# Recurrent mixer: where the projection pieces stand among the five levels of a pair's inversion

## The reference

```python
r, k, v, wd, ad = jnp.split(pf, [W, 2 * W, 3 * W, 3 * W + DECAY_LORA], axis=-1)
w = -jax.nn.softplus(-(w0 + jnp.tanh(wd) @ w2)) - 0.5
decay = jnp.exp(-jnp.exp(w))
a = jax.nn.sigmoid(a0 + ad @ a2)
...
def step(state, inp):                      # 512 steps, 16 heads of 64
    sa = jnp.einsum('bhij,bhj->bhi', state, a_t)
    state = state * w_t[:, :, None, :] + sa[..., None] * b_t[:, :, None, :] + v_t[..., None] * k_t[:, :, None, :]
    return state, jnp.einsum('bhij,bhj->bhi', state, r_t)
...
y = ((y - mean) * lax.rsqrt(var + RWKV_GN_EPS)).reshape(B, S, W) * ln_w + ln_b
```

## Time and profile before

| what | us |
|---|---|
| median of 3 runs (3125.1 to 3125.4) | 3125.38 |
| the profiled execution | 3124.12 |
| its span in the profile | 3122.3 |
| TensorE busy in the span | 3085.4 (99%) |
| VectorE busy | 1768.3 (57%) |
| ScalarE busy | 1274.4 (41%) |

### The profile page before, as it was taken

One profiled execution on the slowest core, in us unless ns is written; L12 is line 12 of the kernel. 1 busy time (PEld: TensorE's weight loads), 2 busy tenths in 40 slices (PEclk: granted clock), 3 DMA queues, 4 the chain that ended last, 5 costly groups with the idle time before them and its releaser, 6 DMA issues. The chain is left out here.

```text
span 3122.3 us, 51762 instructions
## 1 busy us (share of the span) xinstructions
PE 3085.4 (99%) x21393; PEld 2539.7 (81%) x21393; DVE 1768.3 (57%) x3073; ACT 1274.4 (41%) x2328; POOL 215.4 (7%) x170
## 2 busy tenths in 40 slices
PE   8999999999999999999999999999999999999999
PEld 6877777777778778788888888888888888888787
DVE  5335565656666754644457776335556656665822
ACT  4124343434434422524346665323344434443521
POOL 0000000001011101000111121110000000000000
PEclk9999999999999999999999999999999999999999
DMA  8433333342232353343331213534223323332452
GB/s 252 126 81 92 91 88 98 100 115 61 67 98 71 108 176 108 112 106 104 107 102 55 61 55 119 162 108 118 88 81 95 95 75 101 95 95 82 161 164 79
DMA packets 494639, 324.25 MB, mean 104 GB/s; under 512 B 27194, under 2 KB 449693, under 8 KB 494406
## 3 DMA queue, kind: packets, MB, share of 16 engines
q1 hardware_dynamic: 494374, 320.94, 35.1%
q10 hardware_dynamic: 32, 0.01, 0.0%
HBM read 276.05 MB, written 44.85 MB: 103 GB/s over the span
## 5 line engine op out<-in xcount | busy, mean ns | idle before, releaser
L550 DVE TENSOR_TENSOR WLT<-AR,WHT 128x1024 fp32r<-128x1024 f32 (+1 forms) x430 | 527.2, 1232 | 655.7 <-ACT WHT L544 654.9
L562 PE MATMUL PS<-XH,WHT 128*128 128x512 f32 (+1 forms) x2224 | 888.3, 399 | 2.7 <-DVE AR L1045 1.4
L564 PE MATMUL PS<-XH,WLT 128*128 128x512 f32 (+1 forms) x2224 | 867.5, 390 | 0.0
L544 ACT ACTIVATE WHT<-AR 128x1024 fp32r<-128x1024 f32 (+1 forms) x430 | 447.5, 1043 | 597.5 <-PE PS L564 464.1
L563 PE MATMUL PS<-XL,WHT 128*128 128x512 f32 (+1 forms) x1712 | 666.9, 390 | 0.0
L562 PEld LDWEIGHTS PS<-XH,WHT 128*128 128x128 f32 (+1 forms) x2224 | 416.3, 187 | 99.1 <-issue 9.3
L564 PEld LDWEIGHTS PS<-XH,WLT 128*128 128x128 f32 (+1 forms) x2224 | 416.0, 187 | 91.0
L563 PE MATMUL PS<-ARR,WHT 128*128 128x512 f32 x1024 | 398.6, 389 | 0.0
L563 PEld LDWEIGHTS PS<-XL,WHT 128*128 128x128 f32 (+1 forms) x1712 | 320.5, 187 | 66.0 <-issue 2.4
L563 PEld LDWEIGHTS PS<-ARR,WHT 128*128 128x128 f32 x1024 | 192.4, 188 | 39.4 <-issue 0.2
L562 PE MATMUL PS<-XL,WHT 128*128 128x512 f32 x512 | 199.7, 390 | 0.4 <-issue 0.4
(11 more groups left out here) (512 smaller groups left out, 5152.6 us busy)
## 6 DMA issues: line engine op xcount, KB each, us to landing
AR<-b_w_in SPq DMA_DIRECT2D x128, 512.0 KB, 4.0
AR<-w_in SPq DMA_DIRECT2D x122, 512.0 KB, 3.9
AR<-a_w_in SPq DMA_DIRECT2D x48, 512.0 KB, 4.6
AR<-w_out SPq DMA_DIRECT2D x32, 512.0 KB, 4.2
AR<-a_w_out SPq DMA_DIRECT2D x32, 512.0 KB, 3.9
AR<-b_w_out SPq DMA_DIRECT2D x32, 512.0 KB, 4.0
proj_scratch<-AR SPq DMA_DIRECT2D x33, 256.0 KB, 2.1
residual_scratch<-RES SPq DMA_DIRECT2D x8, 1024.0 KB, 6.1
```

The source lines that it names most:

```text
L544: self.nc.scalar.activation(self.shaped(self.high, n), self.shaped(self.raw, n), ACT.Copy).then_inc(self.s_high, 1)
L550: self.nc.vector.tensor_tensor(self.shaped(self.low, n), self.shaped(self.raw, n), f32(self.shaped(self.high, n)), ALU.subtract).then_inc( ...
L562: mm(out, wh, xh[k0 + c], start=(start and c == 0), stop=False)
L564: last = mm(out, wl, xh[k0 + c], start=False, stop=(stop and c == nk - 1))
```

## The change

The two pieces of level 2 go to level 3 and the two of level 4 to level 5. Levels 3 and 5 then have four pieces each, levels 2 and 4 none. The pieces keep their order and number. Nothing else is changed; pairs 6 and 7 keep their own lists.

```diff
-            full = {"start": (0, 1, 2, 3), "x2": (4, 5), "x3": (6, 7), "x4": (8, 9), "x5": (10, 11), "solved": (12,), "h": (13,), "s3": (14, 15)}
+            full = {"start": (0, 1, 2, 3), "x3": (4, 5, 6, 7), "x5": (8, 9, 10, 11), "solved": (12,), "h": (13,), "s3": (14, 15)}
             PIECES = [dict(full) for _ in range(NPAIR - 2)]
             PIECES[0].update(start=(), x1=(0, 1, 2, 3))
```

## The result

| | before | after |
|---|---|---|
| median of 4 runs, us | 3125.39 (3125.1 to 3125.51) | 3157.06 (3156.02 to 3158.87) |
| profiled execution | 3124.12 | 3157.46 |
| its span | 3122.3 | 3155.7 |

The change makes the kernel slower: ratio 1.0102, 95% interval 1.0087 to 1.0118, +31.7 us. Forecast were +18.3 us and a range that ended at 3149.5. The sign was right, the size was not.

The account below looks back on a forecast made before the run. TensorE, busy 99% of the span, was taken to bound the kernel. Moved pieces and new waits for ScalarE summed over pairs 0 to 5 to +18.3 us, giving 3143.7 us, with a range of 3135 to 3149.5.

Parts of the forecast that it names:

- What bounds the kernel: TensorE, busy 99% of the span and idle only 2.87 us in pairs 0 to 5.
- the price of a level: Products to sums of a level on TensorE: 1.16 us with no pieces, 4.02 with two, 6.75 with four.
- Level 2: Bare, its second decay waits for ScalarE's `yc`: products to products 4.60 us instead of 6.17 in pairs 1 to 4.
- Level 4's wait: Bare, line 1599 waits for ScalarE's `sga` until 4.49 us after the products, a 2.35 us stall in pairs 2, 4, 5.
- Nothing gives time back later: Level 5 with four pieces costs +2.73 us; what follows moves along unchanged and gives nothing back.
- The sum of the waits: Pairs 0 to 5 together become 18.3 us longer, between +1.86 and +4.03 us per pair.
- rival 5: Longer stalls halve TensorE's clock for four pieces in each pair: +5.5 us per pair, 33 in all, 3177 us; 2%.
- Rivals 1 to 3: Only level 4's wait real, 3136.6 us (8%); only level 2's, 3130.6 (5%); no waits, fewer shape changes, 3123.5 (5%).
- Rival 4: An unseen further wait, or ScalarE and VectorE work bunching in bare levels: 0.5 to 2 us more per pair, 3152; 8%.

Follow-up runs that it names:

- the seven fillers: Changed kernel plus seven unused 128x512 matmuls before line 1599's wait in level 4 of pairs 0 to 5: 3152.23 us, ratio to before 1.0081.
- the mirror: Kernel before with four pieces each in levels 2 and 4, none in levels 3 and 5: 3137.83 us against 3127.11, ratio 1.0033.
- the gate sigmoid later: Changed kernel with ScalarE's early-tile gate sigmoid in level 4 moved behind the sigmoid that line 1599 waits for: 3150.31 us, ratio to before 1.0068.

## Why the prediction was wrong

**What bounds the kernel, and the price of a level: right.** Bare 1.16 to 1.17 us, four pieces 6.75.

**Level 2: right.** 4.60 and 4.61 us in pairs 1 to 4, 5.27 in pair 5, 3.50 in pair 0, each as computed. (The sums of pair 5, 0.9 us late, were not foreseen and cost nothing.) Half of the change alone gave +5.9 against +6.3.

**Level 4's wait: right in place and length.** Line 1599 starts 4.48 to 4.49 us after the products in pairs 2, 4 and 5, 3.97 in 1 and 3 (computed 4.49 and 3.97), 4.56 in pair 0 (4.68). Taking `sga` forward removed it.

**Nothing gives time back later: right.** From the sums of level 5 to the next pair's first product it is 27.7 us in pairs 1, 3 and 4, before and after.

**The sum of the waits, +18.3: right,** shown by pairs 1 and 3 and by the seven fillers (+18.35, where a measure that scatters by half a us makes the last digits luck).

**The step that failed is rival 5, the clock, at 2%:** in the sum the clock's price stood at nothing. That the clock leaves 1.00 was among the prediction's own signs of being wrong, and it is the one that came. It added 13.3 us, in four of six pairs. I dismissed it with one row, that pair 6 keeps its clock with 3.76 us idle in 47. A mean over 47 us and one instance say little about single waits. Pair 6 itself, whose pieces no run touches, has a fall in 8 of the 13 traces. And the trace of before had a counterexample in it: the fall that begins at 1282.95, behind a wait of 1.0 us, and lasts through one of 1.8 us, both no longer than those that I was about to add six times before line 1599. I never looked for it because the clock of 1.00 was read as a mean. The price that I gave it, 5.5 us in each pair, was too high even for a pair that falls: 2.5 to 4.4 us beyond the forecast wait were measured. The pairs would have been 18.3 us longer without the falls and up to 18.3 + 33 with them; they are 31.6 us longer. The Trainium skill ("TensorE: Matmul & The Clock Gate", "A second HAM failure mode: psum-queue depth-cycling") says that TensorE, idling for very short spells between groups of matmuls often enough, makes its clock swing between the two levels, and that foretold the direction. The section that the prediction named, "HAM oscillation", is about longer idle gaps than any of the new waits and would have let them pass; the falls behind 1.64 us decide against its limit here.

**Rivals 1 to 3** did not occur. Rival 4, work that bunches behind the first wait, is in the experiments only: with line 1773's wait gone, line 1511 waits 0.5 us for the squares.

**What stays open** is which waits the clock falls from. Across these runs it fell behind waits of 1.3 and 1.6 us and not behind one of 2.0, and in the mirror once behind 0.6; the same wait in the same pair fell in one kernel and not in another. No run here separates the length of the wait from what the engine did before it and from the moment at which it came. So the share of pairs that fall could not have been computed from the trace, only that some might.

## What to carry to other kernels

Independent matmuls between two steps of a chain are there for the deadlines of the other engines, not for an even spread: before moving them, follow each engine's program from the last step that it depends on to what TensorE waits for next. Here that gave the two new waits of a pair to within 0.12 us. Then price each new wait twice, once as idle time and once with the clock at half behind it, and look in the trace for single stretches below full clock and at the waits in front of them, never at the mean. Where a wait of one or two microseconds can't be avoided, throwaway matmuls into a free bank are worth a trial: seven made these pairs 13.3 us shorter than the changed kernel's. Whether the whole kernel gains must be measured; with seven it was not clear (ratio to before 1.0081 against 1.0102, overlapping intervals), with three it was just clear (1.0070, whose interval ends at 1.0086, below 1.0087), and where VectorE sets the pace nothing came of it.

## What the runs showed of the hardware

- The clock fell, but not each time, around single idle times of 1.6 to 2.2 us before line 1599, which followed 2.1 us of small matmuls: in 4 of 6 pairs of the changed kernel, 5 of 6 with level 4 alone bare, 4 of 6 with the gate sigmoid later. The fall began between 0.2 us before and 2.3 us after the waiting matmul started and lasted 3.4 to 10.2 us, though big matmuls were running again. A us at half clock cost 0.40 to 0.46 us in these pairs.
- With seven matmuls of 128x512 in this wait, which left at most 0.35 us idle, the clock stayed up in all six pairs; with three, which left 0.75 to 1.27 us, in four of six.
- From the end of ScalarE's sigmoid to the small matmul that waits for it took 0.25 us (line 1773 to 1599, 847.52 to 847.77 in pair 2). From the end of `yc` (line 1834), through the decay that waits for it, to the products of the next level took 1.11 (833.32 to 834.43), where the earlier trace rows gave 1.10.
